# Attention on one Trainium2 core: values stationary and turned probabilities moving, two heads side by side, probabilities divided first, outputs kept turned

## The chip, the core and the metric

The kernel runs on one core of a Trainium2 (trn2) chip. The core has a matrix engine (TensorE, PE in the tables; its loads of the stationary operand are listed as PEld), a vector engine (VectorE, DVE), a scalar engine (ScalarE, ACT), a general engine (GpSimd, POOL) and one that issues transfers (SyncE, SP). Each has its own in-order queue; they wait for each other by semaphores. PE writes into PSUM, eight banks of 512 f32 columns; the rest lies in SBUF, the scratch memory. The metric is the device time of one execution in microseconds, lower is better.

## The reference

Two layers of a hybrid backbone over 128 prompt tokens and 256 latent tokens (three tiles of 128), 1024 wide, all f32. One layer makes q, k, v for three kinds of mixing, two of them softmax attention with heads of 64, then a gated sum of the branches and a mixture of experts. For attention it is, cut down:

```
s  = einsum('bhqd,bhsd->bhqs', q, k) * 64 ** -0.5  (+ bias, mask; kind 2 also a sink column)
pr = softmax(s)                                    # exp(s - max) / sum
o  = einsum('bhqs,bhsd->bqhd', pr, v)              # v: own tokens, for latents also the cached ones
z  = sigmoid(ga) * (o_na @ w_br_na) + sigmoid(gs) * (o_swa @ w_br_swa) + sigmoid(gr) * (o_ret @ w_br_ret)
```

Prompt queries see 128 keys, latent queries 384 (256 latent and 128 cached). There are 8 heads of neighbourhood attention and 4 of window attention. `ga`, `gs`, `gr` are products of the same input with 3072 more columns of `w_in`, the gate product.

## The kernel before, in words

The program is written out by hand for each engine (`nc.Block`, one function each); the order of the code is the order of each queue. All products that must be exact are made of f32 split into a rounded part and a rest: ACT rounds a quarter chunk of weights (`hi_quarter`, L508), DVE makes the rest (`lo_quarter`, L518), PE does three products.

The attention is nine groups of four heads, `GROUPS = [(t, kind) ...]`: kind 0 and 1 are heads 0 to 3 and 4 to 7 of neighbourhood attention, kind 2 the window heads; t is the tile, 0 the prompt, 1 and 2 the latents. So groups 0, 3 and 6 are prompt groups, the others latent ones. Beside them runs the gate product in quarters of twelve products of 128x384 (`gate_quarter`, L855): three in a prompt group, two in a latent one. Each two quarters make one gate tile, to which ACT applies tanh (`gate`, L1998) on its way from bank 7 into `arena`; the first quarter of the next gate tile waits for that tanh.

In a group, PE does the scores of the next group (`scores`, L802), then for each head the transposes of the exponentials (`prob_transposes`, L824) into banks 4 and 5, and, when ACT has copied them to `pT` (`copy`, L1988), the value products (`values`, L839), with the turned probabilities as the stationary and 64 columns of v as the moving operand. DVE adds bias or mask to the scores and takes the maxima (`maxima`, L1365) and, at the group's end, multiplies the sums of four heads in bank 6 by 1/sum on the way into `zt` (`normalise`, L1384 and L1388). ACT does the exponentials with their sums (`exp`, L1976).

After the attention, the rest of the gate product and the retention follow. Then PE turns the outputs of all three branches, 24 transposes (L958), ACT rounds each of the eight turned tiles into `h_hi` (L2036), DVE makes the rests `h_lo` (L1532), and the branch projections begin (L981). `qkT` holds the turned q and k of the heads; the gate tiles lie in columns of `zt` and `qkT` that are no longer needed (`gate_tile`).

Of the kernel before, what the change touches and what calls it, by code (L numbers as in the profile page):

```python
# [13 lines left out]
F32 = mybir.dt.float32  # L14
# [161 lines left out]
def build(nc, a, out):  # L176
    ctx = ExitStack()
    with ctx:
# [17 lines left out]
        def gate_tile(f):  # L196

            if f < 3:
                at = (1, 2, 0)[f] * Z_COLS + KA
            elif f < 18:  # L200
                at = 9216 + (0, 1, 4, 5, 2, 3, 6, 7, 8, 9, 10, 11, 12, 13, 14)[f - 3] * TOK
            elif f < 21:
                at = (f - 18) * Z_COLS + KA + TOK
            else:
                at = (f - 21) * Z_COLS + KR
            return arena[:, at:at + TOK]
# [176 lines left out]
        pv_done = sem("pv_done")  # L383
# [230 lines left out]
        def _(pe):  # L614
# [82 lines left out]
            for l in range(DEPTH):  # L697
# [129 lines left out]
                def values(g, jj):  # L827
                    for t, j, hp, qb, kb, cb, v0, vc in heads_of(g):
                        if j != jj:
                            continue  # L830
                        u = 4 * g + j
                        if j == 0 and g >= 1:
                            pe.wait_ge(o_ready, l * NG + g)
                        pe.wait_ge(pT_ready, l * SU + (u + 1))
                        new = [zt[:, tt, v0:v0 + HD] for tt in (1, 2)]
                        old = cache_v[:, vc, :]
                        vs = {0: [zt[:, 0, v0:v0 + HD]], 1: new + [old], 2: [old] + new}[t]
                        for c, v in enumerate(vs):
# [22 lines left out]
                for g in range(NG):  # L861
                    if g + 1 < NG:
                        scores(g + 1)
                    gate_quarter(i)
                    i += 1
                    prob_transposes(g, 0)
                    for j in range(4):
                        if j < 3:
                            prob_transposes(g, j + 1)
                        values(g, j)  # L870
                        if j in ((0, 2) if GROUPS[g][0] == 0 else (1,)):
                            gate_quarter(i)
                            i += 1
# [81 lines left out]
                for j in range(KT):  # L955
                    c0 = (QA + j * P) if j < 4 else (QS + (j - 4) * P) if j < 6 else QR + (j - 6) * P
# [183 lines left out]
        def _(dve):  # L1140
# [56 lines left out]
            for l in range(DEPTH):  # L1197
# [179 lines left out]
                def normalise(g):  # L1377
                    t, kind = GROUPS[g]
                    dve.wait_ge(exp_ready, l * SU + 4 * g + 4)
                    if kind == 2:  # L1380
# [15 lines left out]
                maxima(0)  # L1396
                i = 2
# [132 lines left out]
                for j in range(KT):  # L1530
                    dve.wait_ge(o_hi, l * KT + j + 1)
                    dve.tensor_tensor(h_lo[:, j, :], ps[:, j, 0:TOK], h_hi[:, j, :].bitcast(F32), ALU.subtract).then_inc(o_lo, 1)  # L1532
# [790 lines left out]
```

## Time and profile before

| what | us |
|---|---|
| median of 3 runs (1333.95 to 1337.48) | 1335.11 |
| the profiled execution | 1337.12 |
| its span, from the first to the last instruction | 1335.2 |
| nine groups of layer 0, from 187.06 to 280.43 | 93.37 |

The profiled execution took 1337.12 us, 1.9 more than its span, and is 2.0 above the median. Times inside an execution are counted from the span's start. Layer 0 ends near 680 us, and layer 1 repeats the same program. The page gives busy time by engine; the chain of waits, followed back from the last instruction, tells what each piece of time was spent on.

### The profile page before, as it was taken

To read this page: it belongs to the slowest core of one execution; us is meant where nothing else is said; L and a number is where in the kernel's file an instruction comes from. 1 tells how busy PE (TensorE), PEld (TensorE's weight loads), DVE (VectorE), ACT (ScalarE), POOL (GpSimd) and SP (SyncE) were. 2 spreads that over 40 slices of the span, in tenths; PEclk is the share of its full clock that TensorE was granted. 3 is DMA by queue.
4 is the path that set the end of the run, shared out by engine and by line. 5 is a ranking of instruction groups with operands and counts; after the bars stand their busy time and mean duration, and the time that the engine had idled before them with its cause. 6 is when DMAs were issued, how large, how long until landed. Compare 5 with 4: busy or idle time off the path is not lost.

```text
span 1335.2 us, 18947 instructions
## 1 busy us (share of the span) xinstructions
PE 1161.0 (87%) x7615; PEld 993.4 (74%) x7615; DVE 663.1 (50%) x1363; ACT 428.7 (32%) x927; POOL 168.6 (13%) x218
## 2 busy tenths in 40 slices
PE   4889999999998779999829999999999876999980
PEld 1667778898897559999727677888998755999970
DVE  2424543434366545665653345344446654665563
ACT  2432244532323303222232233444233330322221
POOL 0031010000011121111022201000002102111102
PEclk9998999999999869999959999999999987999995
DMA  9697661136836238999557976112552624899934
GB/s 320 208 267 204 199 239 64 64 127 226 266 97 236 95 126 295 384 378 375 182 167 216 241 224 206 32 64 68 166 166 88 243 95 132 308 379 375 379 110 162
DMA packets 135401, 272.77 MB, mean 204 GB/s; under 512 B 7184, under 2 KB 89264, under 8 KB 127120
## 3 DMA queue, kind: packets, MB, share of 16 engines
q1 hardware_dynamic: 118992, 219.12, 48.1%
q0 software_dynamic: 15712, 50.79, 12.3%
q10 hardware_dynamic: 608, 1.62, 0.3%
q8 instruction: 62, 1.02, 0.3%
q14 instruction: 27, 0.22, 0.0%
HBM read 249.49 MB, written 22.02 MB: 203 GB/s over the span
## 4 chain that ended last, share of the span: by engine, by line
PE 79%; DVE 8%; DMA 7%; ACT 2%; issue 2%; POOL 1%; SPq 0%; DVEq 0%; POOLq 0%; ACTq 0%
PE ps L1059 17%; PE ps L855 14%; PE ps L730 14%; PE ps L1100 6%; PE ps L981 5%; PE ps L995 5%; DMA ring<-in_w_in 4%; PE ps L839 3%; PE ps L629 3%; DMA ring<-in_ada_w 2%; PE ps L802 2%; PE ps L1051 2%; PE ps L677 1%; PE ps L824 1%; DMA arena<-scratch_ys,slot_i 1%
## 5 line engine op out<-in xcount | busy, mean ns | idle before, releaser
L518 DVE TENSOR_TENSOR w_lo<-ring,w_hi 128x512 fp32r<-128x512 f32 x128 | 88.6, 694 | 205.6 <-ACT w_hi L508 205.6
L521 DVE TENSOR_TENSOR w_lo<-ring,w_hi 128x512 fp32r<-128x512 f32 x128 | 87.9, 692 | 170.0 <-ACT w_hi L510 170.0
L510 ACT ACTIVATE w_hi<-ring 128x512 fp32r<-128x512 f32 x128 | 80.2, 630 | 243.1 <-PE ps L730 152.0
L855 PE MATMUL ps<-h_hi,w_hi 128*128 128x384 f32 x384 | 134.9, 351 | 4.7 <-ACT arena L1998 2.6
L508 ACT ACTIVATE w_hi<-ring 128x512 fp32r<-128x512 f32 x128 | 80.1, 629 | 155.7 <-PE ps L855 85.6
L730 PE MATMUL ps<-w_hi,h_hi 128*128 128x512 f32 x288 | 119.3, 414 | 11.5 <-DVE w_lo L521 8.0
L855 PE MATMUL ps<-h_hi,w_lo 128*128 128x384 f32 x384 | 129.2, 337 | 0.0
L855 PE MATMUL ps<-h_lo,w_hi 128*128 128x384 f32 x384 | 129.1, 336 | 0.0
L730 PE MATMUL ps<-w_lo,h_hi 128*128 128x512 f32 x288 | 115.2, 400 | 0.0
L730 PE MATMUL ps<-w_hi,h_lo 128*128 128x512 f32 x288 | 114.5, 398 | 0.0
L1059 PEld LDWEIGHTS ps<-arena,ring 128*128 128x128 f32 x960 | 109.7, 192 | 1.5
L1059 PE MATMUL ps<-arena,ring 128*128 128x96 f32 x960 | 109.7, 275 | 0.0
L2112 ACT ACTIVATE arena<-ps 128x192 f32<-128x192 f32 x32 | 10.6, 330 | 226.5 <-PE ps L1059 226.5
L855 PEld LDWEIGHTS ps<-h_hi,w_hi 128*128 128x128 f32 x384 | 72.5, 189 | 12.5 <-issue 5.3
L1781 DVE SCALAR_TENSOR_TENSOR arena<-arena,ps 128x192 f32<-128x192 f32 x32 | 11.4, 355 | 139.5 <-ACT arena L2112 139.5
L730 PEld LDWEIGHTS ps<-w_hi,h_hi 128*128 128x128 f32 x288 | 55.6, 193 | 33.3 <-issue 11.5
L629 PE MATMUL ps<-ring,cond 128*32 128x256 f32 x768 | 55.4, 415 | 21.5 <-DMA ring<-in_ada_w 19.9
L1059 PEld LDWEIGHTS ps<-arena 128*128 128x128 f32 x576 | 70.7, 204 | 3.0 <-ACT arena L2082 2.1
L855 PEld LDWEIGHTS ps<-h_lo,w_hi 128*128 128x128 f32 x384 | 72.6, 189 | 0.0
L1059 PE MATMUL ps<-arena 128*128 128x96 f32 x576 | 70.9, 287 | 1.8 <-ACT arena L2082 1.8
L855 PEld LDWEIGHTS ps<-h_hi,w_lo 128*128 128x128 f32 x384 | 72.4, 189 | 0.0
L730 PEld LDWEIGHTS ps<-w_hi,h_lo 128*128 128x128 f32 x288 | 55.7, 193 | 12.5
(296 smaller groups left out, 2239.8 us busy)
## 6 DMA issues: line engine op xcount, KB each, us to landing
ring<-in_ada_w SPq DMA_DIRECT2D x48, 1024.0 KB, 8.9
ring<-in_w_in SPq DMA_DIRECT2D x48, 1024.0 KB, 5.5
ring<-in_w_down SPq DMA_DIRECT2D x18, 1024.0 KB, 9.1
ring<-in_w_up SPq DMA_DIRECT2D x16, 1024.0 KB, 7.6
ring<-in_w_gate SPq DMA_DIRECT2D x14, 1024.0 KB, 8.3
scratch_ys<-arena POOLq DMA_DIRECT2D x30, 384.0 KB, 6.4
arena<-in_w_gate SPq DMA_DIRECT2D x10, 1024.0 KB, 7.7
ring<-in_w_out SPq DMA_DIRECT2D x8, 1024.0 KB, 5.1
```

Source lines behind the costliest of these rows:

```text
L508: eng.activation(gate_weights(w_hi, q), ring[:, slot, k0:k0 + 4, j * P:(j + 1) * P], ACT.Copy).then_inc(whi_ready, 1)
L510: eng.activation(w_hi[:, q % 2], ring[:, slot, 2 * q:2 * q + 2, :], ACT.Copy).then_inc(whi_ready, 1)
L518: eng.tensor_tensor(gate_weights(w_lo, q), ring[:, SLOT[seg, l, c], k0:k0 + 4, j * P:(j + 1) * P], gate_weights(w_hi, q).bitcast(F32), ALU ...
L521: eng.tensor_tensor(w_lo[:, q % 2], ring[:, SLOT[seg, l, c], 2 * q:2 * q + 2, :], w_hi[:, q % 2].bitcast(F32), ALU.subtract).then_inc(wlo_ ...
L629: mm = pe.matmul(ps[g:g + 32, bank, (c % 2) * CH:(c % 2 + 1) * CH], cond32[:, k, :], ring[:, SLOT[item], k, :], start=(k < 4), stop=(k >= ...
L730: mm = pe.matmul(ps[:, b + t, :], hx[:, k, t * P:(t + 1) * P], wx[:, q % 2].rearrange("p k c -> p (k c)"), start=(k == 0 and n == 0), stop ...
L839: mm = pe.matmul(ps[:, 6, j * HD:(j + 1) * HD], pT[:, u % 2, c * P:(c + 1) * P], v, start=(c == 0), stop=(c == len(vs) - 1))
L855: mm = pe.matmul(ps[:, bank, 0:TOK], gate_weights(wx, q)[:, kk, :], hx[:, k, :], start=(k == 0 and n == 0), stop=(k == KT - 1 and n == 2))
L981: mm = pe.matmul(ps[:, bank, 0:TOK], gate_weights(wx, q)[:, kk, :], ox[:, k, :], start=(first and n == 0), stop=(last and n == 2))
L995: mm = pe.matmul(ps[:, 3 * (s // 2) + t, :], zx[:, k, t * P:(t + 1) * P], wx[:, q % 2].rearrange("p k c -> p (k c)"), start=(k == 0 and n ...
L1059: mm = pe.matmul(ps[:, bank, (2 * part + j) * CAP:(2 * part + j + 1) * CAP], w[:, k, j * P:(j + 1) * P], hgT[:, par, k, :], start=(k == 0) ...
L1100: mm = pe.matmul(ps[0:CAP, 4 + 2 * (e % 2) + half, :], a_piece(ax, e % 2)[:, j * CAP:(j + 1) * CAP], down_piece(wx, i), start=(j == 0 and ...
```

## The change

The value products change their operands: v becomes the stationary operand (64 columns) and the turned probabilities the moving one (128 columns). Two heads go to two halves of the array's columns, `tile_position=(0, 0)` and `(0, 64)`, and write rows 0 to 63 and 64 to 127 of bank 6. The output is then turned already (features by tokens), so the division can't be done on it with a factor for each token; the exponentials are multiplied by 1/sum before they are turned, by DVE. The turned outputs are copied into `qkT`, over the q of their own heads, which are no longer needed, and stay turned: six of the eight output tiles need no transposes after the gates. Since `qkT` now holds outputs, the gate tiles get other columns, and the wait for the stored keys and values goes from gate tile 2 to gate tile 5. The order of PE, DVE and ACT in the group is rewritten.

```
             def prob_transposes(g, j):
-                    pe.wait_ge(exp_ready, l * SU + (u + 1))
+                    pe.wait_ge(p_ready, l * SU + (u + 1))
...
-                def values(g, jj):
...
-                            mm = pe.matmul(ps[:, 6, j * HD:(j + 1) * HD], pT[:, u % 2, c * P:(c + 1) * P], v,
-                                           start=(c == 0), stop=(c == len(vs) - 1))
-                        mm.then_inc(pv_done, 1)
+                def values(g, pair):
+                    pe.wait_ge(pT_ready, l * SU + (4 * g + 2 * pair + 2))
+                    if pair == 0 and g >= 1:
+                        pe.wait_ge(o_ready, l * NG + g)
...
+                    for c in range(len(blocks_of[0])):
+                        for n in range(2):
+                            at = HD * n
+                            mm = pe.matmul(ps[at:at + HD, 6, pair * P:(pair + 1) * P], blocks_of[n][c], pT[:, n, c * P:(c + 1) * P],
+                                           start=(c == 0), stop=(c == len(blocks_of[0]) - 1), tile_position=(0, at))
+                    mm.then_inc(pv_done, 1)
...
                 for g in range(NG):
                     if g + 1 < NG:
                         scores(g + 1)
-                    gate_quarter(i)
-                    i += 1
-                    prob_transposes(g, 0)
-                    for j in range(4):
-                        if j < 3:
-                            prob_transposes(g, j + 1)
-                        values(g, j)
-                        if j in ((0, 2) if GROUPS[g][0] == 0 else (1,)):
-                            gate_quarter(i)
-                            i += 1
+                    prompt = GROUPS[g][0] == 0
+                    if prompt:
+                        gate_quarter(i)
+                        i += 1
+                    prob_transposes(g, 0)
+                    prob_transposes(g, 1)
+                    gate_quarter(i)
+                    prob_transposes(g, 2)
+                    values(g, 0)
+                    prob_transposes(g, 3)
+                    gate_quarter(i + 1)
+                    values(g, 1)
+                    i += 2
...
-                for j in range(KT):
+                for j in (6, 7):
...
                 def normalise(g):
...
-                    dve.wait_ge(pv_done, l * SU + 4 * g + 4)
-                    o0 = QA + 256 * kind if kind < 2 else QS
-                    dve.tensor_tensor(zt[:, t, o0:o0 + 256].rearrange("p (h d) -> p h d", d=HD),
-                                      ps[:, 6, 0:256].rearrange("p (h d) -> p h d", d=HD),
-                                      bcast(rden[:, g % 2, :], [P, 4, HD], 2), ALU.mult).then_inc(o_ready, 1)
+                    for j in range(4):
+                        dve.tensor_scalar(sbuf_s[:, g % 2, j, 0:w], sbuf_s[:, g % 2, j, 0:w], rden[:, g % 2, j:j + 1], None,
+                                          ALU.mult).then_inc(p_ready, 1)
+                def output(g):
...
+                    dve.wait_ge(pv_done, l * PV + 2 * g + 2)
+                    dve.tensor_copy(qkT[:, b0:b0 + 2, t * P:(t + 1) * P], ps[:, 6, 0:256].rearrange("p (b q) -> p b q", b=2)
+                                    ).then_inc(o_ready, 1)
...
-                    for n in range(3 if GROUPS[g][0] == 0 else 2):
+                    for n in range(2 if GROUPS[g][0] == 0 else 1):
                         gate_low(i)
                         i += 1
-                    normalise(g)
+                    if g + 1 < NG:
+                        normalise(g + 1)
+                    output(g)
+                    gate_low(i)
+                    i += 1
...
+                done(("g", l, G_CHUNKS - 1))
+                act.wait_ge(o_ready, l * NG + NG)
                 for j in range(KT):
-                    act.wait_ge(ot_psum, l * KT + j + 1)
-                    act.activation(h_hi[:, j, :], ps[:, j, 0:TOK], ACT.Copy).then_inc(o_hi, 1)
+                    if j >= 6:
+                        act.wait_ge(ot_psum, l * 2 + j - 6 + 1)
+                    o = qkT[:, j if j < 4 else j + 4, :] if j < 6 else ps[:, j, 0:TOK]
+                    act.activation(h_hi[:, j, :], o, ACT.Copy).then_inc(o_hi, 1)
```

ACT's order in a latent group was: copy, L508, copy, exponential, copy, exponential, copy, L508, two exponentials; it is now two copies, exponential, L508, copy, exponential, copy, two exponentials, L508, with the tanh behind the L508 that completes a gate tile's weights.

The first place is PE in group 1 of layer 0, the middle of the group. `cst` is the identity (a transpose), `work` the probabilities and their turned copies, `arena` and `cache_v` the values. Before:

```order
L824 MATMUL ps<-cst,work 128x128 x2
L839 MATMUL ps<-arena,work 128x64 [waits pT_ready,o_ready]
L839 MATMUL ps<-arena,work 128x64
L839 MATMUL ps<-cache_v,work 128x64
L824 MATMUL ps<-cst,work 128x128 [waits pT_ready,exp_ready]
L824 MATMUL ps<-cst,work 128x128 x2
L839 MATMUL ps<-arena,work 128x64 [waits pT_ready]
L839 MATMUL ps<-arena,work 128x64
L839 MATMUL ps<-cache_v,work 128x64
L855 MATMUL ps<-h_hi,w_hi 128x384 [waits wlo_ready,gate_ready]
```

The values of one head followed the transposes of the next, and the second quarter (L855) came behind two heads. The same place after the change, between the two quarters:

```order
L824 MATMUL ps<-cst,work 128x128 [waits pT_ready,p_ready]
L824 MATMUL ps<-cst,work 128x128 x2
L841 MATMUL ps<-work,arena 64x128 [waits o_ready,pT_ready]
L841 MATMUL ps<-work,arena 64x128 x3
L841 MATMUL ps<-work,cache_v 64x128 x2
L824 MATMUL ps<-cst,work 128x128 [waits pT_ready,p_ready]
L824 MATMUL ps<-cst,work 128x128 x2
L857 MATMUL ps<-h_hi,w_hi 128x384 [waits wlo_ready,gate_ready]
```

The transposes of heads 0 and 1 have moved ahead of the first quarter, and both heads' values stand together behind the transposes of head 2; the wait for the exponentials has become one for the multiplied probabilities. The second place is DVE in group 1 of layer 0, from the last maxima of group 2 to the first of group 3. Before:

```order
L1365 ISA work,mx<-ps,biasT 128x384 [waits s_psum]
L1365 ISA mx 128x1
L1375 TENSOR_SCALAR nmx<-mx 128x4 [waits s_ready]
L518 TENSOR_TENSOR w_lo<-ring,w_hi 128x512 [waits whi_ready] x2
L1384 RECIPROCAL rden<-den 128x4 [waits exp_ready]
L1388 TENSOR_TENSOR arena<-ps,rden 128x256 [waits pv_done,dve_chain]
L1365 ISA work,mx<-ps,biasT 128x128 [waits s_psum,pt_psum]
```

The reciprocal there is that of group 1. After the change it is that of group 2, whose exponentials follow the maxima just above:

```order
L1370 ISA work,mx<-ps,biasT 128x384 [waits s_psum]
L1370 ISA mx 128x1
L1380 TENSOR_SCALAR nmx<-mx 128x4 [waits s_ready]
L518 TENSOR_TENSOR w_lo<-ring,w_hi 128x512 [waits whi_ready]
L1390 RECIPROCAL rden<-den 128x4 [waits exp_ready]
L1393 TENSOR_SCALAR work<-work,rden 128x384 [waits dve_chain]
L1393 TENSOR_SCALAR work<-work,rden 128x384 x3
L1400 COPY arena<-ps 128x2x128 [waits pv_done]
L518 TENSOR_TENSOR w_lo<-ring,w_hi 128x512 [waits whi_ready]
L1370 ISA work,mx<-ps,biasT 128x128 [waits s_psum,pt_psum]
```

Four multiplications and a copy stand where one multiplication stood, and one of the two splits of weights has moved behind them.

## Rows read from the trace of the kernel before

**Rows 1.** The page: busy time, share and instructions of each engine
```profile
PE 1161.0 (87%) x7615; PEld 993.4 (74%) x7615; DVE 663.1 (50%) x1363; ACT 428.7 (32%) x927; POOL 168.6 (13%) x218
```

**Rows 2.** Chain of waits, layer 0: start us, us, engine and line, instructions
```profile
...
170.66 2.58 PE ps L710 x8
...
177.34 1.00 PE ps L629 x16
...
187.06 1.58 PE ps L802 x16
...
222.78 0.62 ACT w_hi L508
223.83 2.36 PE ps L855 x12
...
260.47 1.51 PE ps L802 x16
261.98 2.29 PE ps L855 x12
264.63 0.50 ACT work L1988
...
267.33 2.15 PE ps L855 x12
269.81 1.46 PE ps L839 x12
...
280.43 1.84 PE ps L880 x16
...
308.25 10.43 DMA ring<-in_w_in
...
```

**Rows 3.** Chain of waits, layer 1: scores in group 7, end of the attention
```profile
...
908.05 1.51 PE ps L802 x16
...
928.01 1.84 PE ps L880 x16
...
```

**Rows 4.** Timeline of ACT in group 7: start us, us, line, form
```profile
...
265.02 0.62 ACT L508 ACTIVATE w_hi<-ring 128x512 fp32r<-128x512 f32 x1
265.54 0.48 ACT L1998 ACTIVATE arena<-ps 128x384 f32<-128x384 f32 x1
265.91 0.49 ACT L1988 ACTIVATE work<-ps 128x384 f32<-128x384 f32 x1
266.28 0.62 ACT L1976 ACTIVATE work<-work,nmx 128x384 f32<-128x384 f32 x1
...
266.87 0.50 ACT L1988 ACTIVATE work<-ps 128x384 f32<-128x384 f32 x1
...
```

**Rows 5.** Timeline of DVE in group 7, same columns
```profile
...
261.00 0.69 DVE L518 TENSOR_TENSOR w_lo<-ring,w_hi 128x512 fp32r<-128x512 f32 x1 [2.77 <-ACT w_hi L508]
...
261.80 0.18 DVE L1384 RECIPROCAL rden<-den 128x4 f32<-128x4 f32 x1
262.02 0.42 DVE L1388 TENSOR_TENSOR arena<-ps,rden 128x256 f32<-128x256 f32 x1
262.36 0.55 DVE L1365 CUSTOM_DVE_ANT_0 work<-ps,cst 128x384 f32<-128x384 f32 x1
...
264.78 0.16 DVE L1373 TENSOR_TENSOR sk<-sink,nmx 128x4 f32<-128x4 f32 x1
...
```

**Rows 6.** Lines by form: count, busy us and mean ns, idle before
```profile
L1248 DVE TENSOR_SCALAR work<-x,rstd 128x1024 f32<-128x1024 f32 x12 | 8.3, 750 | 7.6 <-POOL rstd L2154 7.5
```

**Rows 7.** Chain of waits behind layer 1's gates, columns as in rows 2
```profile
...
998.55 0.50 ACT arena L1998
...
999.67 0.50 ACT h_hi L2036
...
1000.20 1.95 DVE h_lo L1532 x4
...
1004.66 5.47 PE ps L981 x21
```

More of the change, by code:

```diff
@@ L196, in gate_tile @@
         def gate_tile(f):
[L198 to L201, printed above, removed]
+            if f < 12:
+                tile = (1, 2, 0)[f % 3]
+                at = tile * Z_COLS + QA + f // 3 * TOK
             elif f < 21:
-                at = (f - 18) * Z_COLS + KA + TOK
+                at = 9216 + (4, 5, 6, 7, 10, 13, 14, 11, 12)[f - 12] * TOK
             else:
@@ L382, in build @@
         pT_ready = sem("pT_ready")
-        pv_done = sem("pv_done")
+        pv_done, PV = sem("pv_done"), 18
+        p_ready = sem("p_ready")
         o_ready = sem("o_ready")
@@ L825, in prob_transposes @@
                     mm.then_inc(pt_psum, 1)
-                def values(g, jj):
[L828 to L834, printed above, removed]
+                def values(g, pair):
+                    pe.wait_ge(pT_ready, l * SU + (4 * g + 2 * pair + 2))
+                    if pair == 0 and g >= 1:
+                        pe.wait_ge(o_ready, l * NG + g)
+                    heads = list(heads_of(g))[2 * pair:2 * pair + 2]
+                    blocks_of = []
+                    for t, j, hp, qb, kb, cb, v0, vc in heads:
                         new = [zt[:, tt, v0:v0 + HD] for tt in (1, 2)]
                         old = cache_v[:, vc, :]
-                        vs = {0: [zt[:, 0, v0:v0 + HD]], 1: new + [old], 2: [old] + new}[t]
-                        for c, v in enumerate(vs):
-                            mm = pe.matmul(ps[:, 6, j * HD:(j + 1) * HD], pT[:, u % 2, c * P:(c + 1) * P], v,
-                                           start=(c == 0), stop=(c == len(vs) - 1))
-                        mm.then_inc(pv_done, 1)
+                        blocks_of.append({0: [zt[:, 0, v0:v0 + HD]], 1: new + [old], 2: [old] + new}[t])
+                    for c in range(len(blocks_of[0])):
[4 more added lines that the diff above has]
+                    mm.then_inc(pv_done, 1)
                 def gate_quarter(i):
@@ L1378, in normalise @@
                     t, kind = GROUPS[g]
+                    w = P if t == 0 else 384
                     dve.wait_ge(exp_ready, l * SU + 4 * g + 4)
@@ L1396, in _ @@
                 maxima(0)
+                normalise(0)
                 i = 2
@@ L1986, in copy @@
                     if u >= 2:
-                        act.wait_ge(pv_done, l * SU + u - 1)
+                        act.wait_ge(pv_done, l * PV + u // 2)
                     act.activation(pT[:, u % 2, 0:w], ps[:, 4 + u % 2, 0:w], ACT.Copy).then_inc(pT_ready, 1)
                 def gate(f):
-                    if f == 2:
+                    if f == 5:
                         act.wait_ge(kv_stored, l * KV_L + KV_L)
@@ L2011, in _ @@
                     copy(g, 0)
-                    gate_high(i)
-                    copy(g, 1)
-                    for j in range(4):
-                        if g + 1 < NG:
-                            exp(g + 1, j)
-                        if j < 2:
-                            copy(g, j + 2)
-                        if j == 0 and prompt:
-                            gate_high(i + 1)
-                        if j == 1 and not prompt:
-                            gate_high(i + 1)
-                    if prompt:
-                        gate_high(i + 2)
-                    i += 3 if prompt else 2
+                    if prompt:
+                        gate_high(i)
+                        i += 1
+                    copy(g, 1)
+                    if g + 1 < NG:
+                        exp(g + 1, 0)
+                    gate_high(i)
+                    copy(g, 2)
+                    if g + 1 < NG:
+                        exp(g + 1, 1)
+                    copy(g, 3)
+                    if g + 1 < NG:
+                        exp(g + 1, 2)
+                        exp(g + 1, 3)
+                    gate_high(i + 1)
+                    i += 2
                 act.activation(tgr, zt[:, :, GR:GR + 256], ACT.Tanh, scale=0.5).then_inc(tgr_ready, 1)
```

7 lines of the change are left out of this document (5 added, 2 removed).

## The prediction

> **What bounds the kernel now.** I read the shares of busy time first: TensorE (PE) is busy for 87% of the span, VectorE (DVE) for 50%, ScalarE (ACT) for 32% [rows 1]. A share doesn't say which wait ends last in the attention, where the change lies, so I read the chain of waits next, over layer 0's attention [rows 2]. The reader is to see there that nearly every link is a PE instruction: scores (L802), quarters of the gate product (L855), value products (L839). Nine groups of four heads follow each other; group 0 begins with the scores of group 1 at 187.06 and group 8 ends where L880 begins, at 280.43: 93.37 us. Layer 1 is alike: groups 7 and 8 take 928.01 - 908.05 = 19.96 us there and 280.43 - 260.47 = 19.96 here [rows 2, 3].
>
> Group 7 (a latent tile, 384 keys a head) is typical. Scores 1.51, a quarter 2.29 to 264.27, then 3.06 until the second quarter at 267.33: in it lie six transposes, a wait for ACT's copy (L1988, from 264.63), three transposes and the value products of two heads. Then a quarter 2.15, three transposes 0.33, and the value products of the other two heads, 1.46 [rows 2]. So a group lasts 10.80 us, PE-bound with one wait inside it.
>
> **Part one: the value products.** Before, two latent heads are six f32 products, twelve records on PE, in 1.46 us, each of 64 moving columns behind a load of 128 stationary ones. Now a pair of heads is still twelve records, but of 128 moving columns, on two halves of the array. A column costs, by eight records of 384 columns in 2.58 us (L710), 0.84 ns in each record. Twelve records of 128 are 1.29 us one after the other, 0.645 side by side. The score products give the cost of going into a tiled form and out: sixteen records of 3072 columns in all are 2.58 us by that price, 1.29 side by side, and take 1.51: 0.2 over. L629, sixteen records of 256 columns on four column tiles, should take 0.86 and takes 1.00 [rows 2]. So a latent pair costs an estimated 0.645 + 0.2 = **0.85** (from 0.65 with nothing for the switch to 1.49 with nothing side by side); I take 0.85, as both rows of tiled products lie on it. A prompt pair (four records) is 0.21 + 0.2 = 0.42.
>
> L629's row shows that loads of column tiles run beside products in flight: 0.0625 us a record, a quarter of one record's 0.215. The Trainium skill, "TensorE: Matmul & The Clock Gate", Part 3, says that weight loads overlap products in flight only when the row group differs; column tiles share theirs. By that rule no record of a pair would run beside the next one's load; the row speaks against it, and its result is the last rival below.
>
> The order on PE changes too: transposes of heads 0 and 1, quarter, transposes of 2, values of 0 and 1, transposes of 3, quarter, values of 2 and 3. ACT's copies now lie beside quarters, so the wait for L1988 goes. A latent group on PE: scores 1.51 + transposes 6 x 0.11 = 0.67 + quarter 2.2 + 0.33 + 0.85 + 0.33 + 2.2 + 0.85 = **8.95**; followed by a prompt group's scores (eight records of 128 columns, 0.43 + 0.2 = 0.63) **8.1** [rows 2].
>
> **Part two: the added wait.** Transposes no longer wait for the exponentials alone but for DVE, which multiplies the probabilities by 1/sum, and it can do so only when all four exponentials are there. What is queued behind that wait on DVE: the copy of the old group's output, a rest of split weights (L518), and the next group's maxima, for which ACT's next exponentials wait. That closes a ring of ACT and DVE, once round in each group. Its length, from start to start in rows of the latent group 7:
> - ACT [rows 4]: exponential 0.59, rounding of weights (L508) 0.52, copy 0.37, exponential 0.59, copy 0.37, exponential 0.59, the last exponential whole, 0.62: 3.65. A tanh (L1998), 0.37 more, lies between where a gate tile ends there.
> - DVE [rows 5]: reciprocal 0.22, four multiplications, output copy 0.34 (as L1388, start to start), split 0.61, maxima 2.58 in kind 2, from 262.36 to 264.94, and an estimated 2.2 without kind 2's two small steps.
> - The multiplication (128x384, scratch memory to scratch memory, a column as factor) doesn't exist before. The same form of 1024 elements takes 0.750 (L1248) [rows 6]; with the reciprocal of four elements, 0.18, as the fixed part that is 0.56 ns an element: 0.39 for 384, start to start some 0.08 less. Bounds: 0.31 and the maxima's 0.55 on as many elements [rows 5]. I take 0.39, four for 1.25, because L1248 has the same operation and memory.
> Sum 3.65 + 0.22 + 1.25 + 0.34 + 0.61 + 2.2 = 8.3, with tanh 8.65, and some 0.25 for the crossings between engines and the read of the accumulator (an estimate); kind 2 adds 0.4 for maxima and 0.2 for the sink. So in kinds 0 and 1 the ring (8.5 to 8.9) is about as long as PE's 8.95 and costs nothing; in kind 2 (9.1 to 9.5, and the next even quarter waits for the tanh in it) it is **the later one**: I put group 7 at 9.9 (9.5, and 0.4 by which group 6's longer maxima make it start late, an estimate) and group 8, which has no scores to come (8.95 - 1.51 = 7.45), at 7.9, as its first transposes wait for DVE. The further work on DVE is hidden by its idle half.
>
> **Part three: prompt groups.** Here the tanh decides. In group 3 ACT copies, rounds (222.78) and does the tanh after the first quarter, and the next quarter begins only at 223.83 [rows 2]; the change leaves these in that order, and the value products that get cheaper lay in this wait's shadow. Gain 0.1: 10.65. In group 6 both waits get shorter (one copy less ahead of the tanh; transposes alone between the first quarters): 10.8 - 1.05 = 9.75. Group 0 likewise 9.7; its multiplications delay the maxima of group 1, beside a quarter.
>
> Layer sum: 9.7 + 8.95 + 8.1 + 10.65 + 8.95 + 8.1 + 9.75 + 9.9 + 7.9 = 82.0, against 93.37: **11.4 us less**, 22.8 in both.
>
> **Part four: after the gates.** Of 24 transposes six stay, and ACT rounds the outputs from the turned copies, without waiting for PE. Before, the chain is tanh to 999.05, three transposes, rounding 999.67, DVE from 1000.20, and the projections at 1004.66 [rows 7]. ACT can now begin at 999.07: 0.6 earlier. DVE then does the same row of eight subtractions and two splits, so that is all the gain: **0.6 a layer**, 1.2. The removed transposes beyond the first three lay beside DVE's work. The moved gate tiles and the later wait for the stored keys change no duration; those stores are issued before the attention and have 20 us more.
>
> **Sum.** 22.8 + 1.2 = 24.0 from the profiled execution, 1337.12 (its span 1335.2 and 1.9 around it): 1313.1. That execution is 2.0 above the median of the runs, 1335.11, so on the runs' scale **1311**.
>
> **Rivals.**
> 1. *The ring is the bound.* If a multiplication costs the maxima's 0.55 (start to start 0.47 in place of 0.31), the ring grows by 0.64 to 9.2 and 9.5 in kinds 0 and 1: the twelve latent groups lose about 0.6 each, 7 us: **1318**. For it: the operation isn't in the trace. Against: L1248.
> 2. *Pairs don't run side by side.* 1.49 a pair, 0.64 more in 24 latent pairs, 15 us, of which the ring's slack in kind 2 hides little; prompt pairs add 12 x 0.2, half of them beside the tanh: **1327**. Against: L802 and L629.
> 3. *The gain is given back.* Behind the attention of layer 0 the chain goes through a load of w_in for 10.43 us (308.25) [rows 2]. If that landed by its own clock, layer 0's 11.4 would be lost: **1322**. Against: the load is asked for when PE frees its slot, so it moves with PE.
> 4. *Slower.* If each record of a pair waits for its own load and product, as in the skill's rule, the price per record is the 0.215 of a record of 256 columns or more; with 0.275 (load and product one after the other) a latent pair is 12 x 0.275 = 3.3, 2.45 above my 0.85. It decides from 1.85 a pair, where 24 x 1.0 eats the 24 us. At 3.3 it is 24 x 2.45 + 12 x 0.7 = 67 more: **1378**. Against: 0.0625 a record in L629.
>
> **How the numbers follow.** About 0.3% (4 us) is what a measurement of this kernel can tell from no change. Chances: the forecast, 1303 to 1317, 0.60; rival 1 0.17; rival 2 0.08; rival 3 0.05; slower (rival 4, or a ring with waits that I don't see) 0.06; no change, where several of the first three come together, 0.04. All but the last two are faster by over 0.3%: 0.90, within it 0.04, slower 0.06. The range reaches from the pair without switch cost and a shorter ring (some 8 us less, 1303) to rivals 1 and 3 and the lower part of 2: 1303 to 1325.
>
> **What would show it.** In the profile after: a latent pair's twelve records in 0.8 to 0.9 us; no wait for the copies; the multiplication near 0.39; layer 0's nine groups in about 82 us, 7 and 8 with a PE wait for the tanh or for DVE; group 3 unchanged; projections 0.6 us sooner after the last tanh. The prediction is wrong if PE waits for the multiplications in kinds 0 and 1, or if a pair costs over 1.2.

## The result, and the profile after

| | median us | runs | ratio to before, 95% interval |
|---|---|---|---|
| before | 1336.19 | 4 (1333.95 to 1337.48) | |
| changed | 1312.48 | 4 (1311.97 to 1315.3) | 0.9838 (0.9808 to 0.9867) |

The change saves 23.7 us; the forecast was 24.0, to 1311. The profiled execution of the changed kernel took 1315.3 us, its span is 1313.4. A repeat in a later job gave 1311.94; its profiled execution was a disturbed one, so no time of a stage is read from it.

The page's line of busy time, to be held against [rows 1]: PE loses 26 us of work, DVE gains 20, ACT 2.

```profile
PE 1135.4 (86%) x7579; PEld 960.6 (73%) x7579; DVE 683.4 (52%) x1435; ACT 431.0 (33%) x927; POOL 168.8 (13%) x218
```

The chain of waits through group 1 of layer 1 (start us, us, engine and line, instructions), to be held against group 7 in [rows 2]. The reader is to see a chain of nothing but PE: scores, six transposes, a quarter, three transposes, a pair of heads (L841), three transposes, a quarter, a pair. No link is ACT's or DVE's, nor in group 2.

```profile
834.41 1.51 PE ps L802 x16
835.92 0.81 PE ps L824 x6
836.72 2.11 PE ps L857 x12
838.83 0.33 PE ps L824 x3
839.16 0.81 PE ps L841 x12
839.97 0.48 PE ps L824 x3
...
842.53 0.81 PE ps L841 x12
...
```

All groups, in us, from the start of the scores of the next group to that of the one after, by the records of L802. Groups 0, 3 and 6 are prompt groups.

| kernel, layer | 0 | 1 | 2 | 3 | 4 | 5 | 6 | 7 + 8 | sum |
|---|---|---|---|---|---|---|---|---|---|
| before, 0 | 10.77 | 10.80 | 9.95 | 10.77 | 10.56 | 9.67 | 10.82 | 19.87 | 93.21 |
| before, 1 | 12.32 * | 10.80 | 9.94 | 10.74 | 10.55 | 9.70 | 10.79 | 19.87 | 94.71 |
| changed, 0 | 11.50 * | 8.93 | 8.07 | 10.74 | 8.93 | 8.07 | 9.95 | 17.54 | 83.73 |
| changed, 1 | 9.97 | 8.93 | 8.07 | 10.74 | 8.93 | 8.07 | 9.95 | 17.53 | 82.19 |

In the groups with a star PE ran part of the scores and of the first quarter at the lower of its two clock levels (1.2 GHz), for some 1.5 us more; the last section comes back to it. Layer by layer, like with like, the stage went from 93.21 to 82.19: 11.0 us less, where 11.4 was forecast. These starts are 0.1 to 0.2 off those of the chain, in both kernels alike.

Lines by form for layer 0's attention: the new multiplication, and the loads of a pair's values.

```profile
L1393 DVE TENSOR_SCALAR work<-work,rden 128x384 f32<-128x384 f32 x24 | 8.4, 417 | 0.2
L841 PEld LDWEIGHTS ps<-work,arena 128*64 128x64 f32 x104 | 5.6, 136 | 2.7 <-issue 2.7
```

Groups 7 and 8 of layer 1, from group 7's multiplications (L1393) to group 8's. Here the chain does leave PE: from the sums (L1388) through multiplications, output copy, split and maxima on DVE to an exponential and the tanh (L2015) on ACT, and round again to the multiplication that group 8's transposes wait for.

```profile
888.63 0.17 DVE den L1388
...
889.04 0.96 DVE work L1393 x3
...
890.45 0.33 DVE arena L1400
890.78 0.60 DVE w_lo L518
...
893.92 0.71 ACT work L1993 x2
...
895.06 0.46 ACT arena L2015
...
898.68 0.43 DVE work L1393
899.15 0.88 PE ps L824 x6
```

From multiplication to multiplication that is 898.68 - 889.04 = 9.64 us, against PE's 8.93 in a latent group: the ring of ACT and DVE, on whose way round nothing waits for PE, is the later one in kind 2.

Behind the gates of layer 1, to be held against [rows 7]: the rounding (L2059) follows the tanh (L2015) without PE, and DVE begins 978.24 - 977.30 = 0.94 us behind the tanh's start, where it took 1000.20 - 998.55 = 1.65.

```profile
977.30 0.02 ACT arena L2015
...
977.69 0.52 ACT h_hi L2059
978.24 1.96 DVE h_lo L1549 x4
...
982.73 10.51 PE ps L986 x48
```

### The profile page after: what moved, and what is told of

The parts are those of the page before. It is cut to its first block, busy times and chain, and to the rows that moved or that the text cites. A ratio compares the mean times of both kernels' runs of the same rounds, so it can differ in the third digit from the quotient of the medians.

```text
span 1313.4 us, 18931 instructions
## 1 busy us (share of the span) xinstructions
PE 1135.4 (86%) x7579; PEld 960.6 (73%) x7579; DVE 683.4 (52%) x1435; ACT 431.0 (33%) x927; POOL 168.8 (13%) x218
## 3 DMA queue, kind: packets, MB, share of 16 engines
q10 hardware_dynamic: 608, 1.62, 0.3%
## 4 chain that ended last, share of the span: by engine, by line
PE 77%; DVE 9%; DMA 7%; ACT 3%; issue 2%; POOL 1%; SPq 0%; DVEq 0%; ACTq 0%; POOLq 0%
PE ps L1064 17%; PE ps L730 14%; PE ps L857 14%; PE ps L1105 6%; PE ps L986 5%; PE ps L1000 5%; DMA ring<-in_w_in 4%; PE ps L629 3%; DMA ring<-in_ada_w 2%; PE ps L1056 2%; PE ps L802 1%; PE ps L841 1%; PE ps L824 1%; PE ps L677 1%; DMA arena<-scratch_ys,slot_i 1%
## 5 line engine op out<-in xcount | busy, mean ns | idle before, releaser
L508 ACT ACTIVATE w_hi<-ring 128x512 fp32r<-128x512 f32 x128 | 80.0, 628 | 171.0 <-PE ps L857 101.2
L730 PEld LDWEIGHTS ps<-w_hi,h_hi 128*128 128x128 f32 x288 | 55.1, 191 | 35.9 <-issue 11.4
L1798 DVE SCALAR_TENSOR_TENSOR arena<-arena,ps 128x192 f32<-128x192 f32 x32 | 11.4, 355 | 134.6 <-ACT arena L2135 134.6
L629 PE MATMUL ps<-ring,cond 128*32 128x256 f32 x768 | 56.3, 420 | 24.4 <-DMA ring<-in_ada_w 22.9
L1064 PEld LDWEIGHTS ps<-arena 128*128 128x128 f32 x576 | 65.9, 192 | 3.2 <-ACT arena L2105 2.3
L1064 PE MATMUL ps<-arena 128*128 128x96 f32 x576 | 66.1, 275 | 2.0 <-ACT arena L2105 2.0
```

The source lines that it names most:

```text
L508: eng.activation(gate_weights(w_hi, q), ring[:, slot, k0:k0 + 4, j * P:(j + 1) * P], ACT.Copy).then_inc(whi_ready, 1)
L629: mm = pe.matmul(ps[g:g + 32, bank, (c % 2) * CH:(c % 2 + 1) * CH], cond32[:, k, :], ring[:, SLOT[item], k, :], start=(k < 4), stop=(k >= ...
L730: mm = pe.matmul(ps[:, b + t, :], hx[:, k, t * P:(t + 1) * P], wx[:, q % 2].rearrange("p k c -> p (k c)"), start=(k == 0 and n == 0), stop ...
L1064: mm = pe.matmul(ps[:, bank, (2 * part + j) * CAP:(2 * part + j + 1) * CAP], w[:, k, j * P:(j + 1) * P], hgT[:, par, k, :], start=(k == 0) ...
```

## The experiments

The theory is the prediction's: the gain is PE's, from value products side by side and from waits that the new order removes, and the ring of ACT and DVE decides in kind 2 alone. The rivals are that the pairs aren't side by side, that the ring is the bound throughout, and that the new order would do it without the new form. All experiments but one are edits of the changed kernel; the times are medians, the group times come from their traces in the manner of the table above.

### The order alone

The operands of before (turned probabilities stationary, 64 columns of values moving, sums divided at the end, 24 transposes behind the gates), in the order of the changed kernel on PE and ACT; shown against the kernel before, PE's part.

```
-                    gate_quarter(i)
-                    i += 1
-                    prob_transposes(g, 0)
-                    for j in range(4):
-                        if j < 3:
-                            prob_transposes(g, j + 1)
-                        values(g, j)
-                        if j in ((0, 2) if GROUPS[g][0] == 0 else (1,)):
-                            gate_quarter(i)
-                            i += 1
+                    prompt = GROUPS[g][0] == 0
+                    if prompt:
+                        gate_quarter(i)
+                        i += 1
+                    prob_transposes(g, 0)
+                    prob_transposes(g, 1)
+                    gate_quarter(i)
+                    prob_transposes(g, 2)
+                    values(g, 0)
+                    values(g, 1)
+                    prob_transposes(g, 3)
+                    gate_quarter(i + 1)
+                    values(g, 2)
+                    values(g, 3)
+                    i += 2
```

> The kernel before with nothing but the new order of the group on PE and ACT: transposes of two heads, quarter, transposes of the third, values of two heads, transposes of the fourth, quarter, values of two heads. Values, division and the transposes behind the gates are those of before. Theory A (the gain is made of two parts on PE's own path, the order that takes the waits away and the side-by-side values): the latent groups keep 1.46 a pair and go from 10.8 to about 10.1, those at 9.7 to 9.95 to about 9.25, groups 0 and 6 lose about 0.9 each: 5.2 a layer, so about 1326 (1323 to 1329). Rival (the waits were the gain, the form of the values matters little): 1313 to 1317.

Measured: 1318.96 us (1315.57 to 1321.65), ratio 0.9886 (0.9857 to 0.9915). That lies below what my theory gave and above what the rival gave: the order is worth more than I thought, and not everything. The chain of waits of this kernel in group 1 of layer 0, same columns:

```profile
195.37 0.39 PE ps L839 x4
...
200.48 1.29 PE ps L839 x12
201.77 0.33 PE ps L824 x3
...
```

The first row is a prompt group's last two heads. Group 1 takes 9.73 us, 1.07 less than before. What went are the waits for ACT's copies, one of them where I hadn't seen it. In the kernel before two heads' values took 1.46 at 269.81 [rows 2]; the timelines of PE and of ACT there show why:

```profile
270.03 0.39 PE L839 MATMUL ps<-cache_v,work 128*128 128x64 f32 x2
270.38 0.66 PE L839 MATMUL ps<-arena,work 128*128 128x64 f32 x4
```

```profile
269.84 0.49 ACT L1988 ACTIVATE work<-ps 128x384 f32<-128x384 f32 x1 [1.88 <-PE ps L824]
```

The second head starts at 270.38, when the copy of its probabilities has just ended (269.84 + 0.49 = 270.33). So 0.17 of the 1.46 was a wait, and the products alone are 1.29. Against this kernel the new form then saves 2 x (1.29 - 0.81) less 0.15, by which the transposes behind a pair got longer (0.48 for 0.33): 0.81 expected, and 9.73 - 8.93 = 0.80 measured. In groups 7 and 8 the order alone takes 17.73 us, the whole change 17.54: there the products side by side bring almost nothing, since the ring decides, into which the change puts the multiplications.

### Heads in turn

The new form, but all blocks of one head before those of the other, so that records on the two halves no longer alternate.

```
-                    for c in range(len(blocks_of[0])):
-                        for n in range(2):
+                    for n in range(2):
+                        for c in range(len(blocks_of[0])):
```

> The changed kernel with the two heads of a pair written one after the other (all blocks of the first, then all of the second) in place of block by block. Same products, same halves of the array. If the halves work beside each other only because records for both stand near each other in the queue, a latent pair goes from 0.81 to about 1.29 + 0.2 = 1.5 and the time to 1324 to 1328. If each half is fed for itself, whatever the order, 0.81 stays and the time stays within 2 us of 1312.5. I lean to the first.

Measured: 1321.27 us (1319.87 to 1327.71), ratio 0.9927 (0.9899 to 0.9954). The chain of waits in group 1 of layer 0, the first of its two pairs (the second takes 1.07):

```profile
199.89 1.08 PE ps L841 x12
...
```

A pair takes 1.08 instead of 0.81, neither the 1.49 of products one after the other nor the 0.81 of the changed kernel. A latent group takes 9.47, 0.54 more, which is both pairs. So the alternation of the halves is worth a third of a pair's time, and even without it twelve records of 128 columns, at 0.84 ns a column 1.29 us in a row [rows 2], overlap. PE's timeline of that pair shows how:

```profile
200.31 0.27 PE L841 MATMUL ps<-work,cache_v 128*64 128x128 f32 x1
200.36 0.27 PE L841 MATMUL ps<-work,arena 128*64 128x128 f32 x1
200.42 0.27 PE L841 MATMUL ps<-work,cache_v 128*64 128x128 f32 x1
```

Each head has four records on `arena` and then two on `cache_v`, so the row of 200.36 is the second head's and starts between the last two of the first head, ahead of its place in the queue. By the single records of the trace the second head starts 0.27 us behind the first in all twelve latent pairs of that layer, together with the first head's third record, and from there each half goes its own pace, a record every 0.11. The pair is longer by just this 0.27. In the changed kernel the twelve start in twos, 0.007 us apart. Why the second head starts then and not sooner, the records don't tell. The stage accounts for 5.5 of the 8.8 us by which the median lies above the changed kernel's; the rest is not explained.

### Values twice

Each pair's records are issued twice into the same columns, which repeats the same result.

```
+                    for again in range(2):
...
```

> The changed kernel with each pair's value products done twice (the second time over the first's result). It prices the twelve records without the cost of going into and out of the form. Theory A: a latent pair goes from 0.81 to 0.81 + 0.645 = 1.46, prompt pairs from 0.37 to 0.58; the 16 latent pairs of kinds 0 and 1 lie on PE's path and cost 10.3, those of kind 2 up to 5, prompt pairs some 1.5: 1325 to 1329. Rival (the ring of ACT and DVE is the bound in all groups): 1313 to 1317.

Measured: 1329.95 us (1326.67 to 1333.95), ratio 0.9966 (0.9946 to 0.9987), a microsecond above the range expected. The chain of waits, group 1 of layer 0:

```profile
201.96 1.46 PE ps L842 x24
```

Twelve more records add 1.46 - 0.81 = 0.65 us, for which the working gave 0.645 with both halves at work at once. The first twelve cost 0.81, so 0.16 of a pair is the change of form, where I had put 0.2 for going in and out. It isn't the whole of it: the three transposes behind a pair take 0.48 in place of 0.33, another 0.15. A latent group takes 10.24, 1.31 more: nothing hides it. Prompt groups 0, 3 and 6 take 0.21, 0.47 and 0.25 more. So the pairs of group 3 don't lie in the shadow of the tanh.

### The ring longer

DVE does two more multiplications of 128 columns a latent head, into spare columns, ahead of the one that counts.

```
                     for j in range(4):
+                        for again in range(2 if t else 0):
+                            link(dve.tensor_scalar(spare_p, sbuf_s[:, g % 2, j, P * again:P * (again + 1)], rden[:, g % 2, j:j + 1], None,
+                                                   ALU.mult))
+                            linked()
                         dve.tensor_scalar(sbuf_s[:, g % 2, j, 0:w], sbuf_s[:, g % 2, j, 0:w], rden[:, g % 2, j:j + 1], None,
                                           ALU.mult).then_inc(p_ready, 1)
```

> The changed kernel with eight more multiplications of 128 columns on DVE in each latent group, into a spare tile, ahead of the ones that count: about 8 x 0.33 = 2.6 us more on the ring, nothing more on PE. Theory A: in kinds 0 and 1 the ring (8.5 to 8.9) is about as long as PE's 8.95, so all but 0.1 to 0.4 of the 2.6 shows where two latent groups follow each other (groups 1, 4, 7), less behind prompt groups: about 9 us a layer, 1326 to 1334. Rival (the ring has slack of a microsecond or more): under 1320.

Measured: 1336.33 us (1333.17 to 1341.51), ratio 1.0031 (1.0011 to 1.0051): the whole gain is gone, and 2 us more than I expected at the most. DVE's timeline from group 4 to group 5 of layer 1 gives the dose (the spare pair is L1395, the multiplication that counts L1398):

```profile
871.50 0.61 DVE L1395 TENSOR_SCALAR arena<-work,rden 128x128 f32<-128x128 f32 x2
872.14 0.42 DVE L1398 TENSOR_SCALAR work<-work,rden 128x384 f32<-128x384 f32 x1
...
882.59 0.61 DVE L1395 TENSOR_SCALAR arena<-work,rden 128x128 f32<-128x128 f32 x2
```

A spare pair takes 872.14 - 871.50 = 0.64 from start to start, so the ring grows by 2.56 a latent group. Groups 7 and 8 together take 4.2 and 4.7 more in the two layers (in the second with a stretch at the lower clock), most of twice the dose: little slack. Groups 4 and 5 take 1.5 and 1.9 more (10.41 and 9.99), so PE had 1.1 and 0.6 in hand there. These aren't the time by which the ring is shorter than PE's 8.93: from 871.50 to 882.59 it goes round in 11.09, so in 8.53 without the dose. They are a lead that the multiplications have behind a prompt group. The changed kernel shows the same lead, in the timeline of DVE and the chain of waits for groups 4 and 5 of layer 1:

```profile
861.98 1.41 DVE L1393 TENSOR_SCALAR work<-work,rden 128x384 f32<-128x384 f32 x4
870.71 1.41 DVE L1393 TENSOR_SCALAR work<-work,rden 128x384 f32<-128x384 f32 x4
```

```profile
863.66 0.81 PE ps L824 x6
...
871.72 0.81 PE ps L824 x6
```

The first of each four multiplications takes 0.42, so it ends at 862.40 and 871.13, 1.3 and 0.6 before the transposes (L824) that need it.

In group 1 the loss is 4.0, more than the dose. PE's timeline there, in layer 0, shows a wait for the tanh that the longer ring delays:

```profile
205.58 0.45 PE L857 MATMUL ps<-h_hi,w_hi 128*128 128x384 f32 x1 [2.28 <-ACT arena L2020]
```

The windows of the same place (length; busy time of PE, PEld, DVE, ACT and POOL; PE's granted clock; DMA share; GB/s) show what the records run at:

```profile
204.00:206.00 2.00, 0.42 (x2) 0.42 (x3) 0.69 (x1) 2.00 (x6) 0.00 (x0) 1.00 1.05 374
...
208.00:210.00 2.00, 2.00 (x15) 1.32 (x13) 1.72 (x7) 0.70 (x2) 0.00 (x0) 0.50 0.00 0
```

PE is idle for 2.28 us, and some microsecond behind its return the granted clock falls to 0.50, the level of 1.2 GHz: it is 0.73, 0.50 and 0.92 in the three stretches from 206 to 212, which is 1.7 us of full clock less. The 2.28 and the 1.7 make the 4.0: this wait of PE is paid for twice.

### Tanh first

In the attention ACT does the tanh of a finished gate tile before it rounds the next weights, not behind.

```
                 def gate_high(i):

+                    if i % 2 == 1 and i < IN_ATTENTION + 2:
+                        gate(i // 2 - 1)
                     hi_quarter(act, l, "g", i // 4, i % 4)
-                    if i % 2 == 1:
+                    if i % 2 == 1 and i >= IN_ATTENTION + 2:
                         gate(i // 2 - 1)
```

> The changed kernel with ACT's tanh of a gate tile ahead of the rounding of weights (L508) that completes the next one's weights, within the attention; both wait for the same quarter of PE. Theory A (PE's waits in the prompt groups end with the tanh, and what lies ahead of it on ACT prolongs them): about 0.5 less in each of groups 0, 3 and 6 and 0.3 to 0.5 in group 7: 4 us less in both layers, about 1308.5. Rival (the split weights end these waits, not the tanh): 1312 to 1313.

Measured: 1310.4 us (1308.1 to 1316.46), ratio 0.9839 (0.9804 to 0.9875). Groups 0, 3 and 6 lose the 0.5 us that L508 takes, as expected (9.43 for 9.95 in group 6). But groups 7 and 8 take 18.07 for 17.53, where I had expected 0.3 to 0.5 less, and groups 6 to 8 together 27.50 for 27.48; so the 4 us forecast didn't come. What group 6 gains is only waited for later: the ring of kind 2 sets the end of the three.

### Division head by head

DVE takes reciprocal and multiplication of each head as soon as its exponential is there, not when all four are; ACT does the sink's exponential ahead of the first one.

```
-                    dve.wait_ge(exp_ready, l * SU + 4 * g + 4)
...
+                    for j in range(4):
+                        dve.wait_ge(exp_ready, l * SU + 4 * g + j + 1)
+                        one = den[:, g % 2, j:j + 1]
...
+                        link(dve.reciprocal(rden[:, g % 2, j:j + 1], one))
+                        linked()
+                        dve.tensor_scalar(sbuf_s[:, g % 2, j, 0:w], sbuf_s[:, g % 2, j, 0:w], rden[:, g % 2, j:j + 1], None,
+                                          ALU.mult).then_inc(p_ready, 1)
```

> The changed kernel with reciprocal and multiplication done head by head as its own exponential ends, and the sink's exponential ahead of the four. The ring gets about 0.9 to 1.2 shorter where it matters (behind the last exponential come one sum, one reciprocal and one multiplication in place of four). Theory A: PE bounds kinds 0 and 1, so nothing there; groups 7 and 8 lose their waits, 1.2 to 1.6 a layer: about 1310 (1309 to 1311). Rival (ring the bound in all latent groups): 1304 or less.

Measured: 1310.02 us (1304.74 to 1313.68), ratio 0.983 (0.9793 to 0.9867). Groups 7 and 8 take 16.34 us, 1.2 less, and none of groups 1 to 6 moves by more than 0.02 (group 0 has a star in both layers). The chain of waits in group 8 of layer 0, to the first work behind the attention, is PE alone again, from the transposes that waited for DVE:

```profile
259.93 0.81 PE ps L824 x6
...
267.35 1.98 PE ps L885 x16
```

So the added wait for all four exponentials, with the sink's exponential (0.10) behind the fourth, cost 1.2 us in groups 7 and 8, and nothing in kinds 0 and 1, where PE is the later one.

### Both orders together

The last two edits in one kernel, and a third: the first group's multiplications stand behind the maxima of group 1, not ahead of them. It was run twice, the second time in one job with the changed kernel.

```
                 maxima(0)
-                normalise(0)
...
                         maxima(g + 1)
+                    if g == 0:
+                        normalise(0)
```

> Tanh first and head by head together, and the first group's multiplications behind the maxima of group 1 in place of ahead of them (0.3 in group 0). Theory A: the three lie in different places and add: 1305 (1303 to 1308). Rival (they share one wait): 1308 to 1310.

> The changed kernel with both orders of the earlier runs (tanh ahead of the weights of the same quarter; division head by head), again beside the changed one. If the stage tells, 80.0 us a layer against 82.2, so 4.4 us less than the changed kernel in the same job: 1307 to 1308. If the gain is only noise between jobs, the two come out alike.

> The changed kernel once more, beside the next one on the same chip. 1312 us, 1309 to 1315, ratio to before 0.983 to 0.984. Its nine groups take 82.2 us a layer, or 83.7 where group 0 of a layer runs its first quarter at half clock; if that half clock belongs to layer 0 of this kernel, it is there again, if it comes by the run, it need not be.

Measured: 1305.92 us, ratio 0.9797 (0.976 to 0.9834), and 1308.37 (1305.72 to 1310.48), ratio 0.9832 (0.98 to 0.9865), in the job in which the changed kernel took 1311.94, ratio 0.9859 (0.9827 to 0.9891). The stage takes 79.98 us against 82.19, so 4.4 less in two layers; the second job's medians are 3.6 apart. The intervals overlap, so the times alone don't settle it; the stage does, with 79.98 to 79.99 in the three layers without a starred group. Of the 0.5 us of group 6 (9.43) some 0.3 is still given back: groups 7 and 8 take 16.66, with the division head by head alone 16.34. And the third edit, for which I expected 0.3 in group 0, shows no gain: that group with a star takes 11.02, with the tanh first alone 11.01 and 11.03.

## Why the prediction was right, point by point

**The value pair** was put at 0.85 and takes 0.81; a prompt pair 0.37, for 0.42. The working from L710, L802 and L629 [rows 2] held, and the doubled values confirm its part of 0.65 for columns; rival 2 falls with it. The switch is 0.16 in the pair, for 0.2, and 0.15 more behind it, which my sum didn't have. The last rival, by the load rule in the Trainium skill, "TensorE: Matmul & The Clock Gate", Part 3 (loads overlap products in flight only with another row group), didn't come: each of the twelve records has a load of 136 ns, which alone would be 1.63 us in a row, and the twelve take 0.81. The trace doesn't agree with that rule for two column tiles, nor for the old form: in the kernel with the order alone twelve loads of 192 ns, 2.3 in a row, stand beside products that take 1.29. That rival's price was loose as well: 0.275 a record stands in no row as a load and a product in a row, which with 136 ns and the 0.84 ns of 128 columns would be 0.244, 2.9 a pair.

**The latent group** was put at 8.95 and takes 8.93; with a prompt group's scores 8.07, for 8.1. The path was right; that the total fits so closely is luck, as its parts missed both ways: six transposes 0.81 for 0.67 and the three behind a pair 0.48 for 0.33, against the two quarters 4.2 for 4.4 and the two pairs 1.62 for 1.70. The first two lie behind products on parts of the array, and what they take more is the cost of coming out of that form. [Rows 2] had it: a quarter takes 2.29 behind the scores and 2.15 behind value products.

The split of the gain was wrong. I read the whole 1.46 of an old pair as products, where 0.17 was a wait for ACT, and I didn't see the 0.15 that the new form adds behind it. So I thought the larger part of the gain to be the new form's. The runs show otherwise: without the starred quarters the order alone takes 85.6 us a layer (87.10 less 1.5), of the 11.0 us it brings 7.6. This is also why I missed the time of the order alone.

**The added wait.** A multiplication takes 417 ns, 320 from start to start (0.96 for three); 390 and 310 were the estimates, between bounds whose upper end would have made rival 1. The ring comes round in 9.64 us in kind 2, with 9.1 to 9.5 forecast, and decides there: groups 7 and 8 take 17.5, for 17.8. In kinds 0 and 1 I put it at 8.5 to 8.9, "about as long as PE's 8.95", and that is what it is: 870.71 - 861.98 = 8.73 from group 4's multiplications to group 5's, and 8.53 by the longer ring. But the 8.95 was the wrong measure. As the scores of the prompt group to come are short, PE asks for group 5's probabilities 871.72 - 863.66 = 8.06 after group 4's, sooner than the ring comes round. That it costs nothing is due to the lead of 1.3 us that the longer prompt group before them leaves, of which 0.6 is left over; I hadn't counted either. In kind 2 the same sum gives the price: group 8 has no scores, so PE asks 8.93 - 1.51 = 7.42 after group 7's first transposes; the ring takes 9.64, the lead is 1.1 (the first multiplication ends at 889.04 + 0.42, the transposes start at 890.53), and 1.1 us remain, for 1.2 that the division head by head gets back. Rival 1 falls for kinds 0 and 1 and holds for kind 2 alone, as forecast.

**Prompt groups.** 9.97, 10.74 and 9.95, for 9.7, 10.65 and 9.75. The tanh's wait stands in group 3 as it stood before:

```profile
855.52 0.62 ACT w_hi L508
856.14 0.39 ACT arena L2015
856.57 2.35 PE ps L857 x12
859.04 0.37 PE ps L841 x4
```

The kernel with the tanh first shows the price, 0.5 a prompt group. The reason I gave for group 3's small gain was wrong: its pairs come behind that wait, not in its shadow, and doubling them costs 0.47. They bring nothing because two old heads take 0.39 in the new order (the row of L839 x4 above), and the new pair 0.37: what is saved in columns goes into the switch. Groups 0 and 6 gained from the order, as it alone gives 9.98 in group 6.

**Behind the gates** 0.6 a layer was forecast. From the tanh to the projections layer 1 takes 982.73 - 977.30 = 5.43, for 1004.66 - 998.55 = 6.11: 0.68. In layer 0 PE has one more product of the conditioning (L629, with the weights `in_ada_w`) to do behind its last gate product, and the transposes waited for what DVE makes of it. The chain of waits there, before and then after the change, from that product's end to the next work on PE:

```profile
361.85 0.86 issue
...
368.26 0.64 PE ps L640 x8
```

```profile
357.20 0.02 issue
...
362.31 1.08 PE ps L640 x8
```

That is 5.11 for 6.41, a gain of 1.30: the tanh and the first roundings now lie beside that product, where the transposes couldn't begin before its end. I had read layer 1 and carried it over. Both layers: 2.0, for 1.2.

**Rival 3** falls. The load behind layer 0's attention moves with PE and is waited for nearly as long:

```profile
274.38 1.98 PE ps L885 x16
...
302.34 11.20 DMA ring<-in_w_in
```

From the attention's end it is 302.34 - 274.38 = 27.96 us to this wait, before 27.82 [rows 2]. The wait is 0.8 longer: of layer 0's gain that much is given back, not all.

**The sum.** Two stages of 11.0 and the tails' 2.0 make 24.0, the forecast's sum from parts of which the stages were 0.8 too large and the tails 0.8 too small; that these cancel is luck. The two profiled spans differ by 21.8, as the changed kernel's attention began 3.5 us later in its execution (190.58, for 187.06), ahead of what the change touches; in other runs of its order it began at 184 to 188.

## What to carry to other kernels

A record with a moving side of 64 columns took 0.107 us here (1.29 for twelve), twice what its columns come to at 0.84 ns; whether the 64 columns or the load of 128 ahead of them set this, no run here separates. Swap the operands so that the wide side moves, put two heads on two halves of the array, and write their records alternately; and count what the transposes or products behind that form pay for leaving it. But look first for what an idle wait beside the products costs: here two thirds of the stage's gain came from putting another engine's copies beside long products, which needs no new form. And where a change adds a step between two engines that feed each other, add up the whole ring once round and hold it against the time after which the bound engine asks again, for each pair of groups that follow each other: it costs nothing until it is the longer one and the lead from a longer group ahead is used up, and then all of it.

## What the runs showed of the hardware

Twelve records on two halves of the array take 0.81 us when the halves alternate and 1.08 when one half's six records come first. In the second case the other half's records start 0.27 us behind the first's, among them and ahead of their place in the queue: for products on two halves PE's queue isn't strictly in order. Three transposes behind a pair in this form take 0.48 us, behind products on the whole array 0.33. Why the second half starts after just 0.27, and why leaving the form costs 0.15, the records don't tell.

The starred quarters come by the execution, not by the kernel. The kernel with both orders had none in its first profile (9.68 in group 0 of layer 0) and one in its second (11.01). The windows there, from the idle time of PE ahead of the attention on, first profile and then second, columns as above:

```profile
180.00:184.00 4.00, 1.86 (x19) 1.43 (x17) 3.27 (x13) 1.02 (x3) 2.54 (x4) 1.00 1.07 350
184.00:188.00 4.00, 3.75 (x29) 3.48 (x29) 3.05 (x16) 1.65 (x8) 0.00 (x0) 1.00 1.02 411
```

```profile
183.00:187.00 4.00, 2.10 (x21) 1.67 (x19) 3.27 (x11) 1.25 (x3) 2.76 (x4) 1.00 1.07 348
187.00:191.00 4.00, 3.51 (x20) 3.09 (x21) 2.70 (x16) 1.65 (x8) 0.00 (x0) 0.64 1.01 403
```

In both PE has work for half of the 4 us ahead of the attention, while it waits for DVE. Behind that the granted clock stays at 1.00 in the one and is 0.64 in the other. In the profiles read here each group with a star has such idle time ahead of it, but not each such idle time is followed by the lower level; what decides isn't seen. A stage that begins behind an idle PE is best compared in a layer without it.
